# The order of expert dots, weights and sums at the start of a product-key expert stage, and the order of its row buffers

## The chip, the cores and the metric

The kernel is one program on one NeuronCore of a Trainium2 chip. The metric is the device time of one launch in microseconds (us). Three runs of the kernel before took 2640.28 us in the median (2638.99 to 2640.45). A core has five engines that matter here: TensorE (PE) for matrix products, VectorE (DVE), ScalarE (ACT), GpSimd (POOL) and SyncE (SP). Each runs its own list of instructions in order and waits for others at semaphores. Sixteen DMA engines move data between device memory and the on-chip memory.

## What is computed

Two blocks follow each other on 256 tokens of width 1024. The change touches only the end of the second one, a product-key expert layer:

```
q = (xc @ peer_wq).reshape(PEER_CHUNK, PEER_HEADS, 2, PEER_QDIM // 2)
s = jnp.einsum('chpd,hpkd->chpk', q, peer_keys)
sv, si = lax.top_k(s, PEER_TOPK)                       # 16 of 128 keys, twice per head
cand = sv[..., 0, :, None] + sv[..., 1, None, :]       # 256 pairs
top_s, pos = lax.top_k(cand, PEER_TOPK)                # 16 experts per head
gate = jax.nn.softmax(top_s, axis=-1)
act = jax.nn.gelu(jnp.einsum('chkd,cd->chk', peer_u[eidx], xc))
return jnp.einsum('chk,chkd->cd', (gate * act), peer_v[eidx])
```

There are 8 heads with 16 chosen experts each, so each token needs 128 rows of `peer_u` and 128 of `peer_v`, 1024 numbers in each. All is float32.

## The kernel before

The tokens are two tiles of 128 (t = 0 and 1). One "row" n, from 0 to 255, is one chosen expert of each of the 128 tokens of a tile: n = 128 t + 16 h + k for head h and choice k. A row is one indirect DMA (line 3484, issued by POOL) which gathers for each token 8 KB, its row of u and its row of v side by side, into one of 16 row buffers. Four rows are a group (`SLOT_GROUPS`, group b holds rows 4b to 4b+3), so there are 64 groups.

Each row goes through four engines:

- POOL issues the gather when its buffer is free, that is when the row that used it last has been summed (`rows_summed`).
- DVE multiplies the u half with the token (`slot_dots`, line 3324).
- ACT makes the gated activation and from it a diagonal matrix (`slot_weight`, lines 2713 to 2724, the diagonal is the last of them).
- PE multiplies the diagonal with the v half and adds to the output (`sums`, line 2379).

Ahead of the gathers stands the choice of the experts. PE computes queries (`tile_queries` for one tile, `query_chunk` for both tiles, line 1890) with four weight blocks of 2 MB, wq0 to wq3 (heads 0 and 1, 2 and 3, 4 and 5, 6 and 7), ACT copies them (lines 2683, 2689), PE computes the key scores, ACT copies these (line 2695), and DVE ranks (`rank`, from line 3236; `pair_up`, line 3253; `rank_pairs`, from line 3261; `choose`, from line 3292). `expert_gates` (ACT line 2708, DVE line 3312) is the softmax. The units of choice are: head 0 of tile 0, head 1 of tile 0, then two heads at a time. Unit 1 must be chosen before row 16 is gathered, unit 2 before row 32, unit 3 before row 64.

The four engines run lists written out by hand, and each list mixes the groups with the queries and scores of later heads. In the kernel before:

- DVE chooses unit 0 and unit 1, then takes group 0, group 1, `rank(2)`, group 2, the rest of unit 2 between groups 2, 3 and 4, and unit 3 between groups 8 to 12.
- ACT makes the weights of group 0 after the last query copy of wq1, groups 1 and 2 after the scores of wq1, then takes the copy of tile 1's wq0 queries, group 3, scores, groups 4 and 5, `query_pair(2, 0)`, groups 6 and 7, `query_pair(2, 1)`, group 8, `key_scores(2)`, group 9 and so on.
- PE sums groups 0 to 2 after the scores of wq1, then computes tile 1's wq0 queries, sums group 3, and then alternates one `query_chunk` of wq2 and wq3 with one group, 4+c and 8+c.

Buffers 0 to 4 are free at once, buffer 5 after tile 1's normalised input has been transposed, buffers 6 and 7 lie in the memory of wq1 and are free after its last query copy, buffers 8 and 9 lie in the memory of wq2 and are lent to rows 5 and 6 before wq2 is loaded, and come back after wq2's queries. Buffers 10 to 15 become free later. So after the first ten rows the gathers of rows 10 to 41 run with eight buffers. SP loads wq2 after row 6 is summed, and wq3 after tile 1's transposes (`h2_transposes(1)`).

Of the kernel before, what the change touches and what calls it, by code (L numbers as in the profile page):

```python
# [332 lines left out]
def build_program(nc, W1, V1, K1, W2_all, VV2, K2, R2, PU, PV, xin, cin, out):  # L333
# [1394 lines left out]
    behind_scores = [free2, free2 + 2 * D, free2 + 8 * D]  # L1728
    row_at = free_at_once + [behind_norm] + behind_query[1] + behind_query[2] + behind_query[3] + behind_scores
    NBUF = len(row_at)  # L1730
    first_bufs = [*range(5), 8, 9, 5, 6, 7] + [*range(8)] * 4 + [8, 9, *range(8)] * 2
    BEFORE_QUERY = [5, 6]
    cycle = [*range(8, 16), *range(8)]
    buf_of = (first_bufs + cycle * (TT * P // NBUF))[:TT * P]
    uses_before = [buf_of[:n].count(buf_of[n]) for n in range(TT * P)]
    user_before = [max((m for m in range(n) if buf_of[m] == buf_of[n]), default=None) for n in range(TT * P)]
# [140 lines left out]
    def _(pe):  # L1877
# [503 lines left out]
                        if half == 1 or n == TT * P - 1:  # L2381
                            last.then_inc(rows_summed.sem, 1)

        SCORED = {0: (0, 4), 1: (2, 3), 2: (5, 5), 3: (6, 6)}

        def score_products(g, t, chunks=range(4)):
            b = act_ring.open(pe, "sp")
# [36 lines left out]
        item_now["fresh"] = False  # L2424
        tile_queries(wq1, 0)
        tile_transposes(1)
        pe.wait_ge(*hT2_by_act.at(0, 3))
        tile_queries(wq1, 1)
        key_scores(1)
        sums([0, 1, 2])  # L2430
        tile_queries(wq0, 1)
        sums([3])
        key_scores(0, (1,))
        h2_transposes(1)
        pe.drain().then_inc(weights.used, 1)
        for c in range(4):
            query_chunk(2, c)
            sums([4 + c])
        key_scores(2)
        for c in range(4):  # L2440
            query_chunk(3, c)
            sums([8 + c])
        key_scores(3)
        sums(range(12, len(SLOT_GROUPS)))


    @block.scalar
    def _(act):
# [277 lines left out]
        def slot_weights(groups):  # L2726
            for b in groups:
                for n in range(*SLOT_GROUPS[b]):
                    slot_weight(n)
                if b % 8 == 3 and b // 8 + 2 < len(UNITS):  # L2730
                    expert_gates(b // 8 + 2)

        tile_root(0)
# [7 lines left out]
        expert_gates(0)  # L2741
        tile_queries(1, 0)
        tile_evac(1)
        expert_gates(1)
        tile_queries(1, 1)
        slot_weights([0])
        key_scores(1)
        slot_weights([1, 2])
        tile_queries(0, 1)
        slot_weights([3])  # L2750
        key_scores(0, (1,))
        h2_copies(1)
        slot_weights([4, 5])
        query_pair(2, 0)
        slot_weights([6, 7])
        query_pair(2, 1)
# [13 lines left out]
    def _(v):  # L2770
# [574 lines left out]
        choose_first(0)  # L3345
        add_out(1, 1)
        tile_norm(1)
        choose_first(1)
        expert_gates(0)
        expert_gates(1)  # L3350
        v.wait_ge(*h2_ready.at(0, 0))
        for b in range(len(SLOT_GROUPS)):
            if SLOT_GROUPS[b][0] == P:
                v.wait_ge(*h2_ready.at(0, 1))
            slot_dots(b)
            ahead = b // 8 + 2
            if ahead < len(UNITS):
                phase = b % 8 - (ahead == 2)
                if phase == 0:
                    rank(ahead)  # L3360
                elif phase == 1:
                    pair_up(ahead)
                    rank_pairs(ahead)
                elif phase == 2:
                    choose(ahead)
                elif b % 8 == 4:
                    expert_gates(ahead)
            if b == 36:
                add_experts(0)
# [4 lines left out]
    @block.gpsimd  # L3374
    def _(pool):
        layers_pool(pool)
        def ptt(o, a, b, op):
            return pool.tensor_tensor(o, a, b, op)  # L3378

        def unit_keys(h, d, dst, factor):  # L3380
            t = slice(starts(h)[d], starts(h)[d] + 64)
            if h:
                ptt(dst, kk[:, :, t], factor, ALU.mult)
            else:
                ptt(dst[:, 0:4, :], kk[:, 0:4, t], factor[:, 0:4, :], ALU.mult)
                ptt(dst[:, 4:8, :], kk_late[:, :, t], factor[:, 4:8, :], ALU.mult)

        def removal_raw(h):
            for d in range(2):
                unit_keys(h, d, ch2(Pm)[:, d, :, :], R1[h % 2][:, d, :, :])  # L3390
            pool.drain()

        def key_factors(h):
            for d in range(2):
                a = R1[h % 2][:, d, :, :]
                ptt(a, a, bc(V2["k_a"], 2, 64), ALU.mult)
            pool.drain()
            for d in range(2):
                a = R1[h % 2][:, d, :, :]
                ptt(a, a, bc(ka_rest, 2, 64), ALU.add)  # L3400
            pool.drain()

        def removal_keys(h):
            pool.wait_ge(*decays_ready.at(h))
            for head in range(2):
                rows_ = slice(64 * head, 64 * head + 64)
                ptt(QK[rows_, :, head, :], ch(Pm)[rows_, :, :], ch(r2)[rows_, :, :], ALU.mult)
            pool.drain()
            for d in range(2):
                unit_keys(h, d, ch2(Pm)[:, d, :, :], R0_before[h % 2][d])  # L3410
            pool.drain().then_inc(pq_ready.sem, 1)

        def keys_raw(h):
            for d in range(2):
                a = R1[h % 2][:, d, :, :]
                ptt(a, a, zk[:, :, starts(h)[d]:starts(h)[d] + 64], ALU.mult)
            pool.drain()

        def keys(h):
            raw = R1[h % 2].rearrange("p d c n -> p (d c) n")  # L3420
            for head in range(2):
                rows_ = slice(64 * head, 64 * head + 64)
                ptt(QK[rows_, :, 1 - head, :], raw[rows_, :, :], ch(r2)[rows_, :, :], ALU.mult)
            pool.drain().then_inc(k_ready.sem, 1)

        def begin_inverse(h):
            first = C2["level"].rearrange("p (m d t) -> p m d t", m=LEVELS + 1, d=2)[:, 0, :, :]
            for d in range(2):
                pool.wait_ge(*intra_ready.at(h, d))
                if h:  # L3430
                    pool.wait_ge(*u_ready.at(h - 1, d))
                for head in range(2):
                    rows_ = slice(64 * head, 64 * head + 64)
                    ptt(ch2(DTm)[rows_, d, :, :], ch2(LA[head])[rows_, d, :, :], bc(first[rows_, d, :], 1, 8), ALU.mult)
                pool.drain().then_inc(inverseT_ready[d].sem, 1)  # L3435

        for pair in range(8):
            d, c = divmod(2 * pair, 8)
            pool.wait_ge(*cumsum_ready.at(0, pair))
            for part in range(2):  # L3440
                pool.dma_start(rates_dram[d, :, :, part, c:c + 2, :].rearrange("b p c n -> p b (c n)"),  # L3441
                               staged[pair % 3][part].rearrange("p b c n -> p b (c n)")).then_inc(rates_stored[pair % 3], 16)
        pool.wait_ge(*kk_ready.at(0))
        pool.wait_ge(rates_landed[0], 64)
        pool.wait_ge(weights.used, used0 + SLOTS + LAST_BEFORE_SCAN + 1)
        removal_raw(0)
        key_factors(0)
        removal_keys(0)
        keys_raw(0)
        keys(0)  # L3450
        for h in STEPS:
            begin_inverse(h)
            if h == 0:
                pool.tensor_copy(kk[:, 4:8, :], kk_late)
                pool.drain()
            if h < 7:
                pool.wait_ge(rates_landed[(h + 1) % 2], 64 * ((h + 1) // 2 + 1))
                act_ring.peek(pool, "post", "U0", 2 * h + 1)
                if h in X_STEPS:
                    dve_ring.peek(pool, "post", "reads1", 2 * (h - 4) + 1)  # L3460
                removal_raw(h + 1)
                key_factors(h + 1)
                removal_keys(h + 1)
                keys_raw(h + 1)
                keys(h + 1)

        for n in range(TT * P):
            if n in UNIT_AT:
                pool.wait_ge(*experts_ready.at(0, UNIT_AT[n]))
            m, at = user_before[n], row_at[buf_of[n]]  # L3470
            if m is None and at == behind_norm:
                pool.wait_ge(*hT2_by_act.at(0, 3))
            for g, done in ((1, 3), (3, 6)):
                if m is None and at == behind_query[g][0]:
                    pool.wait_ge(*qTp_ready.at(0, done))
            if n == BEFORE_QUERY[0]:
                pool.wait_ge(weights.used, used0 + SLOTS + ITEM2["wq0"] + 1)
            elif m == BEFORE_QUERY[0]:
                pool.wait_ge(*qTp_ready.at(0, 5))
            if m is None and at == behind_scores[0]:  # L3480
                pool.wait_ge(*scores_ready.at(0, 8))
            if m is not None:
                pool.wait_ge(*rows_summed.at(0, m))
            pool.indirect_dma_start(out=rows_uv[buf_of[n]], out_offset=None, in_=UV,  # L3484
                                    in_offset=bass.IndirectOffsetOnAxis(ap=eidx_u[:, n:n + 1], axis=0)).then_inc(row_landed[buf_of[n]], 16)
# [32 lines left out]
```

## Time and profile before

| | |
|---|---|
| median of three runs | 2640.28 us |
| profiled execution, its own time | 2640.01 us |
| its span in the profile | 2638.1 us |
| PE busy | 2438.0 us (92%) |
| DVE busy | 1509.2 us (57%) |
| ACT busy | 899.9 us (34%) |
| POOL busy | 649.6 us (25%) |
| gathers of rows | 256, from 1960.0 to 2593.5 us |

The profile's page divides the span into 40 equal slices, 66 us each. The expert stage is the last ten of them. In the rows below a busy time has its own column, and the engine's idle time ahead of an instruction stands in brackets with what ended it: `[10.83 <-PE psum L2379]` says that the engine stood still for 10.83 us until an instruction of line 2379 on PE had finished. Line 2780 is a helper through which many DVE products and sums are issued.

### The profile page before, as it was taken

To read this page: it belongs to the slowest core of one execution; us is meant where nothing else is said; L and a number is where in the kernel's file an instruction comes from. 1 tells how busy PE (TensorE), PEld (TensorE's weight loads), DVE (VectorE), ACT (ScalarE), POOL (GpSimd) and SP (SyncE) were. 2 spreads that over 40 slices of the span, in tenths; PEclk is the share of its full clock that TensorE was granted. 3 is DMA by queue.
4 is the path that set the end of the run, shared out by engine and by line. 5 is a ranking of instruction groups with operands and counts; after the bars stand their busy time and mean duration, and the time that the engine had idled before them with its cause. 6 is when DMAs were issued, how large, how long until landed. Compare 5 with 4: busy or idle time off the path is not lost.

```text
span 2638.1 us, 48116 instructions
## 1 busy us (share of the span) xinstructions
PE 2438.0 (92%) x19036; PEld 1682.9 (64%) x19036; DVE 1509.2 (57%) x2848; ACT 899.9 (34%) x2505; POOL 649.6 (25%) x512
## 2 busy tenths in 40 slices
PE   8999999999999999999999888989999987877787
PEld 6588696476887954845677778888865532322232
DVE  1874376537734755576457445455056666677654
ACT  1252100013330000016332333221016676766676
POOL 0000014300000242000014657440013454444551
PEclk9999999999999999999999999999999999999999
DMA  4432444344234545215432111003449999999997
GB/s 186 156 128 97 160 160 160 147 175 150 106 124 180 224 160 206 114 64 224 158 130 64 34 23 30 19 34 137 159 181 393 414 421 421 421 422 421 421 421 301
DMA packets 91686, 523.98 MB, mean 199 GB/s; under 512 B 39776, under 2 KB 39776, under 8 KB 43488
## 3 DMA queue, kind: packets, MB, share of 16 engines
q0 software_dynamic: 39360, 277.51, 25.7%
q1 hardware_dynamic: 52128, 243.80, 24.8%
q8 instruction: 127, 2.08, 0.3%
q14 instruction: 71, 0.58, 0.1%
HBM read 511.85 MB, written 9.44 MB: 198 GB/s over the span
## 4 chain that ended last, share of the span: by engine, by line
PE 68%; DVE 11%; DMA 10%; issue 5%; ACT 3%; POOL 1%; POOLq 1%; DVEq 1%; ACTq 1%; PEldq 0%; SPq 0%
PE psum L571 34%; PE psum L1890 23%; DMA mem<-weights,mem 10%; PE psum L2379 5%; DVE mem L2780 4%; DVE mem L3324 3%; PE psum L813 2%; PE psum L587 1%; POOL mem L3378 1%; PE psum L2347 1%; DVE mem L3131 1%; PE psum L1900 1%; POOLq L3435 1%; ACT mem L2724 0%; ACT mem L2720 0%
## 5 line engine op out<-in xcount | busy, mean ns | idle before, releaser
L1890 PE MATMUL psum<-mem 64*64 64x64 f32 (+6 forms) x12356 | 874.4, 265 | 53.9 <-DVEq L3135 14.7
L571 PE MATMUL psum<-mem 128*128 128x128 f32 (+9 forms) x4856 | 910.4, 359 | 11.2 <-DVE mem L1198 3.5
L1890 PEld LDWEIGHTS psum<-mem 64*64 64x64 f32 (+4 forms) x12356 | 710.3, 151 | 208.1 <-issue 124.5
L571 PEld LDWEIGHTS psum<-mem 128*128 128x128 f32 (+4 forms) x4856 | 685.4, 183 | 230.5 <-issue 158.1
L2379 PE MATMUL psum<-mem 128*128 128x512 f32 x1024 | 505.3, 633 | 108.2 <-ACT mem L2724 108.0
L2379 PEld LDWEIGHTS psum<-mem 128*128 128x128 f32 x1024 | 187.5, 197 | 419.4 <-ACT mem L2724 259.2
L3324 DVE CUSTOM_DVE_ANT_0 mem<-mem 128x1024 f32<-128x1024 f32 x256 | 314.1, 1227 | 208.0 <-DMA mem<-weights,mem 191.3
L3484 POOL DMA_INDIRECT mem<-weights,mem x256 | 295.1, 1153 | 537.1 <-PE psum L2379 310.3
L2780 DVE TENSOR_TENSOR mem<-psum,mem 128x512 f32<-128x512 f32 (+2 forms) x180 | 111.5, 630 | 254.8 <-PE psum L1890 228.2
L3378 POOL TENSOR_TENSOR mem<-mem 128x512 f32<-128x512 f32 (+3 forms) x148 | 205.7, 1402 | 153.7 <-DVEq L3100 120.2
L2780 DVE TENSOR_TENSOR mem<-mem 128x512 f32<-128x512 f32 (+4 forms) x154 | 135.4, 893 | 11.8 <-ACTq L2540 2.2
L1552 POOL TENSOR_TENSOR mem<-mem 128x1024 f32<-128x1024 f32 x14 | 26.9, 1924 | 460.3 <-ACTq L1102 460.3
L1263 DVE SCALAR_TENSOR_TENSOR mem<-mem 128x256 f32<-128x256 f32 x240 | 105.6, 481 | 9.0 <-issue 0.4
L2724 ACT ACTIVATE mem<-mem 128x128 f32<-128x128 f32 x256 | 102.8, 402 | 18.5 <-issue 0.7
L2720 ACT ACTIVATE mem<-mem 128x1 f32<-128x1 f32 x256 | 99.1, 387 | 18.4 <-issue 0.3
L2715 ACT ACTIVATE mem<-mem 128x1 f32<-128x1 f32 x256 | 99.1, 387 | 18.1 <-issue 0.3
L3441 POOL DMA_DIRECT2D rates_dram<-mem x16 | 14.2, 891 | 366.8 <-DVEq L3018 366.8
L2642 ACT ACTIVATE mem<-psum 128x512 f32<-128x512 f32 x80 | 47.7, 597 | 130.6 <-PE psum L1890 130.6
L2713 ACT ACTIVATE mem<-mem 128x1 f32<-128x1 f32 x256 | 49.8, 195 | 119.8 <-DVEq L3325 118.8
L949 ACT ACTIVATE mem<-psum 128x512 f32<-128x512 f32 (+4 forms) x88 | 45.6, 569 | 104.4 <-PE psum L571 100.2
L1563 POOL MEMSET mem<- 128x256 f32 x1 | 0.3, 305 | 319.3 <-ACT mem L1097 319.3
L1101 ACT ACTIVATE mem<-mem 128x1024 f32<-128x1024 f32 x14 | 14.8, 1058 | 168.4 <-DVEq L1199 168.4
(284 smaller groups left out, 1791.9 us busy)
## 6 DMA issues: line engine op xcount, KB each, us to landing
mem<-weights SPq DMA_DIRECT2D x97, 2048.0 KB, 7.3
mem<-weights SPq DMA_DIRECT2D x13, 1024.0 KB, 9.9
rates_dram<-mem POOLq DMA_DIRECT2D x16, 512.0 KB, 5.0
mem<-rates_dram SPq DMA_DIRECT2D x32, 256.0 KB, 4.6
mem<-weights SPq DMA_DIRECT2D x2, 2176.0 KB, 7.9
mem<-weights,mem POOLq DMA_INDIRECT x256, 30.8
mem<-weights SPq DMA_DIRECT2D x2, 1536.0 KB, 8.1
mem<-weights SPq DMA_DIRECT2D x2, 1152.0 KB, 8.8
```

What stands on the lines that cost most here:

```text
L571: ins = pe.matmul(out, lhsT, rhs, start=start, stop=stop, skip_group_check=skip)
L813: ins = pe.matmul(b, mg[:, k, t * P:(t + 1) * P], w[half][:, k, :], start=k == 0, stop=k == 7)
L1263: v.scalar_tensor_tensor(cacc[:, c, :], src, w, cacc[:, c, :], ALU.mult, ALU.add)
L1890: ins = pe.matmul(out, lhsT, rhs, start=start, stop=stop, skip_group_check=skip)
L2379: last = pe.matmul(psum[:, 4 + 2 * t + half, :], diag[:, n % DIAGS, :], rows_uv[buf_of[n]][:, D + half * 512:D + (half + 1) * 512], start= ...
L2715: A(w, w, ACT.Identity, scale=dot, bias=dot)
L2720: A(w, w, ACT.Identity, scale=dot, bias=dot)
L2724: A(diag[:, n % DIAGS, :], ident, ACT.Copy, scale=w).then_inc(diag_ready.sem, 1)
L2780: return v.tensor_tensor(o, a, b, op)
L3324: v.tensor_tensor_reduce(u, u, h2[:, n // P, :], 1.0, 0.0, ALU.mult, ALU.add, actp[:, n:n + 1])
L3378: return pool.tensor_tensor(o, a, b, op)
L3484: pool.indirect_dma_start(out=rows_uv[buf_of[n]], out_offset=None, in_=UV, in_offset=bass.IndirectOffsetOnAxis(ap=eidx_u[:, n:n + 1], axis ...
```

## The change

PE, ACT and DVE get other lists for the first groups, and the row buffers are used in another order. No instruction's work is changed, except that one query product of 512 columns and its copy are cut into two halves.

- DVE takes group 0 after `rank(1)`, group 1 after `rank_pairs(1)`, and only then `choose(1)` and `expert_gates(1)`. Group 2 follows, then `rank(2)`; unit 2 lies one group later than before.
- ACT takes group 0 ahead of the copy of tile 1's wq1 queries, group 1 ahead of the scores of wq1, and group 2 behind `expert_gates(1)`. The copy of tile 1's wq0 queries is halved, with group 3 between the halves and group 4 behind. From `query_pair(2, 0)` on ACT's list is as before.
- PE sums group 0 ahead of tile 1's wq1 queries, group 1 ahead of the scores of wq1, group 2 behind them, group 3 between the halves of tile 1's wq0 queries and group 4 behind. From there on each `query_chunk` is followed by the group 5+c or 9+c, one later than before.
- Buffers 6 and 7 are used first by rows 11 and 12, not by rows 8 and 9. Rows 8, 9 and 10 take buffers 0, 1 and 2 again.

```diff
-    first_bufs = [*range(5), 8, 9, 5, 6, 7] + [*range(8)] * 4 + [8, 9, *range(8)] * 2
+    eight = [0, 1, 2, 6, 7, 3, 4, 5]
+    first_bufs = [*range(5), 8, 9, 5] + eight * 4 + [8, 9, *eight] * 2
-    cycle = [*range(8, 16), *range(8)]
+    cycle = [*range(8, 16), *eight]
...
         tile_queries(wq1, 0)
         tile_transposes(1)
+        sums([0])
         pe.wait_ge(*hT2_by_act.at(0, 3))
         tile_queries(wq1, 1)
+        sums([1])
         key_scores(1)
-        sums([0, 1, 2])
-        tile_queries(wq0, 1)
+        sums([2])
+        tile_queries(wq0, 1, (0, 1))
         sums([3])
+        tile_queries(wq0, 1, (2, 3))
+        sums([4])
         key_scores(0, (1,))
         h2_transposes(1)
         pe.drain().then_inc(weights.used, 1)
         for c in range(4):
             query_chunk(2, c)
-            sums([4 + c])
+            sums([5 + c])
         key_scores(2)
         for c in range(4):
             query_chunk(3, c)
-            sums([8 + c])
+            sums([9 + c])
         key_scores(3)
-        sums(range(12, len(SLOT_GROUPS)))
+        sums(range(13, len(SLOT_GROUPS)))
...
-                if b % 8 == 3 and b // 8 + 2 < len(UNITS):
+                if b % 8 == (3 if b >= 8 else 5) and b // 8 + 2 < len(UNITS):
                     expert_gates(b // 8 + 2)
...
         tile_evac(1)
+        slot_weights([0])
+        tile_queries(1, 1)
+        slot_weights([1])
+        key_scores(1)
         expert_gates(1)
-        tile_queries(1, 1)
-        slot_weights([0])
-        key_scores(1)
-        slot_weights([1, 2])
-        tile_queries(0, 1)
+        slot_weights([2])
+        tile_queries(0, 1, 0, 2)
         slot_weights([3])
+        tile_queries(0, 1, 2, 4)
+        slot_weights([4])
         key_scores(0, (1,))
         h2_copies(1)
-        slot_weights([4, 5])
+        slot_weights([5])
         query_pair(2, 0)
         slot_weights([6, 7])
         query_pair(2, 1)
...
-        choose_first(1)
+        rank(1)
         expert_gates(0)
+        v.wait_ge(*h2_ready.at(0, 0))
+        slot_dots(0)
+        pair_up(1)
+        rank_pairs(1)
+        slot_dots(1)
+        choose(1)
         expert_gates(1)
-        v.wait_ge(*h2_ready.at(0, 0))
-        for b in range(len(SLOT_GROUPS)):
+        for b in range(2, len(SLOT_GROUPS)):
...
-                phase = b % 8 - (ahead == 2)
+                phase = b % 8 - (2 if ahead == 2 else 0)
```

The remaining lines of the diff move the indices of `qTp_ready` by one, since the halved copy signals twice.

## Rows read from the trace of the kernel before

**Rows 1.** The page, 40 slices: busy tenths and GB/s of the DMA engines

```profile
DMA  4432444344234545215432111003449999999997
GB/s 186 156 128 97 160 160 160 147 175 150 106 124 180 224 160 206 114 64 224 158 130 64 34 23 30 19 34 137 159 181 393 414 421 421 421 422 421 421 421 301
```

**Rows 2.** Busy time by stretch: engines with instruction counts, PE's granted clock, DMA share, GB/s

```profile
1972.00:1974.00 2.00, 2.00 (x11) 2.00 (x11) 1.65 (x5) 0.00 (x0) 0.00 (x0) 0.50 1.01 426
...
2018.00:2020.00 2.00, 2.00 (x5) 0.68 (x4) 1.74 (x3) 1.73 (x7) 1.31 (x1) 1.00 0.06 25
2020.00:2022.00 2.00, 2.00 (x5) 0.68 (x4) 1.84 (x3) 1.72 (x7) 1.09 (x2) 1.00 0.65 143
...
2020.00:2060.00 40.00, 39.74 (x133) 23.80 (x133) 16.56 (x30) 29.35 (x102) 15.66 (x16) 1.00 0.99 399
...
2100.00:2200.00 100.00, 86.81 (x199) 35.46 (x197) 70.04 (x159) 72.22 (x257) 51.23 (x48) 0.95 1.01 421
```

**Rows 3.** DVE in order of time, the dot of the last row

```profile
2628.23 1.23 DVE L3324 CUSTOM_DVE_ANT_0 mem<-mem 128x1024 f32<-128x1024 f32 x1 [1.22 <-DMA mem<-weights,mem]
```

**Rows 4.** POOL in order of time: start, duration; issues of rows 0, 8 and 20

```profile
1960.03 1.07 POOL L3484 DMA_INDIRECT mem<-weights,mem  x1 [197.34 <-DVE mem L3303]
...
1979.87 0.95 POOL L3484 DMA_INDIRECT mem<-weights,mem  x1 [8.82 <-ACTq L2685]
...
2018.69 1.45 POOL L3484 DMA_INDIRECT mem<-weights,mem  x1 [10.83 <-PE psum L2379]
```

**Rows 5.** DVE in order of time, 1963 to 2025 us

```profile
1963.98 0.49 DVE L3236 MAX8 mem<-mem 128x8 f32<-128x128 f32 x2
...
1967.01 0.18 DVE L3253 CAST mem<-mem 128x32 f32<-128x32 uint32 x1
...
1970.12 0.20 DVE L3292 TENSOR_SCALAR mem<-mem 128x16 uint32<-128x16 uint32 x1
...
1974.40 0.17 DVE L3312 TENSOR_REDUCE mem<-mem 128x1 f32<-128x16 f32 x1
...
1975.97 1.22 DVE L3324 CUSTOM_DVE_ANT_0 mem<-mem 128x1024 f32<-128x1024 f32 x1 [0.18 <-issue]
1977.36 1.23 DVE L3324 CUSTOM_DVE_ANT_0 mem<-mem 128x1024 f32<-128x1024 f32 x1 [0.16 <-issue]
...
1988.08 0.87 DVE L3236 MAX8 mem<-mem 128x8 f32<-128x128 f32 x4 [1.13 <-ACTq L2697]
...
1993.62 1.23 DVE L3324 CUSTOM_DVE_ANT_0 mem<-mem 128x1024 f32<-128x1024 f32 x1
...
2024.76 1.23 DVE L3324 CUSTOM_DVE_ANT_0 mem<-mem 128x1024 f32<-128x1024 f32 x1 [1.72 <-DMA mem<-weights,mem]
```

**Rows 6.** ACT in order of time: query copies and the first weights

```profile
1978.97 0.60 ACT L2683 ACTIVATE mem<-psum 128x512 f32<-128x512 f32 x1 [4.41 <-PE psum L1890]
1979.68 0.20 ACT L2713 ACTIVATE mem<-mem 128x1 f32<-128x1 f32 x1
...
1981.33 0.40 ACT L2724 ACTIVATE mem<-mem 128x128 f32<-128x128 f32 x1
...
1983.26 0.40 ACT L2724 ACTIVATE mem<-mem 128x128 f32<-128x128 f32 x1
...
2013.63 0.60 ACT L2683 ACTIVATE mem<-psum 128x512 f32<-128x512 f32 x1 [9.22 <-PE psum L1890]
```

**Rows 7.** PE in order of time: queries and scores L1890, sums L2379

```profile
1969.89 10.92 PE L1890 MATMUL psum<-mem 128*128 128x128 f32 x80 [2.86 <-ACTq L2680]
...
2006.29 7.31 PE L1890 MATMUL psum<-mem 128*128 128x128 f32 x64
...
2067.74 5.40 PE L1890 MATMUL psum<-mem 128*128 128x128 f32 x32
2072.98 7.03 PE L2379 MATMUL psum<-mem 128*128 128x512 f32 x16
2079.84 3.62 PE L1890 MATMUL psum<-mem 128*128 128x256 f32 x16
```

More of the change, by code:

```diff
@@ L2382, in sums @@
                             last.then_inc(rows_summed.sem, 1)
-        SCORED = {0: (0, 4), 1: (2, 3), 2: (5, 5), 3: (6, 6)}
+        SCORED = {0: (0, 5), 1: (2, 3), 2: (6, 6), 3: (7, 7)}
         def score_products(g, t, chunks=range(4)):
@@ L3365, in _ @@
                     choose(ahead)
-                elif b % 8 == 4:
+                elif phase == 4:
                     expert_gates(ahead)
@@ L3472, in _ @@
                 pool.wait_ge(*hT2_by_act.at(0, 3))
-            for g, done in ((1, 3), (3, 6)):
+            for g, done in ((1, 3), (3, 7)):
                 if m is None and at == behind_query[g][0]:
@@ L3478, in _ @@
             elif m == BEFORE_QUERY[0]:
-                pool.wait_ge(*qTp_ready.at(0, 5))
+                pool.wait_ge(*qTp_ready.at(0, 6))
             if m is None and at == behind_scores[0]:
```

## The prediction, made before the changed kernel was run

> **What bounds the kernel now.** I read the page's slices first [rows 1]. From the 31st slice on, 1979 us, the DMA engines are full at 414 to 422 GB/s to the end. The stretches say the same more sharply: share 1.01 and 421 GB/s in 2100 to 2200 us [rows 2]. A row is 128 x 8 KB = 1.049 MB, so it costs 1.049 MB / 421 GB/s = 2.49 us, and 256 rows are 637 us of the 678 us that lie between the first gather [rows 4] and the end. The last dot waits for a gather too [rows 3]. So the expert stage is bound by DMA from its first gather to its last, and only two things can move the time: when the first gather starts, and how long the DMA engines stand empty in between.
>
> The first gather starts at 1960.03, released by `choose(0)` [rows 4]. The change puts nothing ahead of that. Inside the stage I looked for stretches under full share. There is one: 0.06 and 0.65 in 2018 to 2022 [rows 2], that is 1.9 + 0.7 = 2.6 us of standstill. It is the wait of row 20 for its buffer: POOL idle for 10.83 us until a sum on PE had ended, issue at 2018.69 [rows 4]. Behind it stand ACT, idle 9.22 us until the copy at 2013.63 [rows 6], and PE, which had to finish 7.31 us of queries from 2006.29 first [rows 7]. After the hole the gathers depend on PE: it is busy 39.74 of 40 us in 2020 to 2060 [rows 2], with sums of 7.03 us and query pieces of 3.62 us end to end [rows 7].
>
> **What the change can gain.** The hole and no more: 2.6 us, with its edges about 3. That would give 2640.0 - 3 = 2637. What the trace doesn't show is the changed order itself, so I lay the four lists out by hand with durations of this profile.
>
> **Unit costs.** A dot 1.39 us, from start to start [rows 5]. The first diagonal is ready 1981.33 + 0.40 - 1979.68 = 2.05 us after ACT begins, each further one 1.93 us later [rows 6]. A group of sums takes 7.03 us with ready diagonals, 4 x 1.93 = 7.7 at ACT's pace. `rank(1)` 3.0, `rank_pairs(1)` 3.1, `choose(1)` with its gate shift 4.3, `rank(2)` 5.5 us, by the differences of starts [rows 5]. A query product of 512 columns 7.31 us, a chunk of both tiles 3.6, two score products 5.40 - 3.6 = 1.8, so 0.9 each [rows 7]; a copy 0.6 [rows 6]. From issue to the dot of a row on an empty queue 2024.76 - 2018.69 = 6.1 us [rows 4, 5], so row n lands at about 1966 + 2.5 n at first. Two further numbers concern the queue. A weight block is 2.1 MB, two rows. And the pace at which rows come to the dots is a little slower than 2.49: from row 20 to row 255 with wq3 between, (2628.23 - 2024.76) / 237 = 2.55 us [rows 3, 5]. I use 2.55.
>
> **The first three groups.** DVE: dots of group 0 from 1967.8, paced by the landings until 1975, then 3.1 us of pairs, group 1 until row 7 has landed, 1985, `choose(1)` until 1989. ACT has finished tile 1's transposed copies at 1969.9 (where PE's wait of 2.86 us ended, [rows 7]); weights of group 0 from 1970 to 1978. PE sums them 1972 to 1979.7. Only then come tile 1's wq1 queries, 7.3 us, before at 1969.89 [rows 7], now until 1987; copy until 1987.6. Row 11, the first in the wq1 buffers, is issued then. The rows ahead of it, 0 to 10, keep the queue full until about 1962 + 11 x 2.5 = 1989.5, so this is just in time: cost 0 to 1 us. Weights of group 1, ready since 1979, now stand behind that copy: 1987.6 to 1995.4, sums until 1997, two scores until 1998.8, copies until 1999.3. ACT's `expert_gates(1)` is behind them and DVE waits for it before group 2: dots from 2000.3, where they were at 1993.62 [rows 5]. `rank(2)` no longer stands ahead of them, which gives 5.5 us of DVE back, but DVE has idled 11 us. Sums of group 2 run from 2003.7 to 2011.2, half a query until 2014.8, copy and first weight, sums of group 3 from 2017.3. Row 20 waits for row 12 as before, so the hole stays: issue at 2019.5 instead of 2018.69, 3 us empty.
>
> **The loop behind.** Here is the dearest part. From `query_pair(2, 0)` on ACT's list is unchanged, while PE has moved one group forward. Before, group 5 is weighted ahead of the copy of the first wq2 pair and summed behind it, so PE finds its diagonals ready and never stops. After, the sums of group 6 come directly behind chunk 1, whose copy stands ahead of ACT's group 6: PE waits 0.6 + 2.05 = 2.65 us, and again at groups 8, 10 and 12; the halved query costs 0.4 + 2.05 at groups 3 and 4 in the same way. The scores of wq2 stand behind the sums of group 8 and not of 7, and `rank(3)`, which waits for them, stands ahead of the dots of group 9: scores copied at 2090, rank until 2095.7, dots, weights, sums from 2099. Written out, the sums of groups 3 to 12 begin at 2017.3, 2030.8, 2043.9, 2057.3, 2068.2, 2081.3, 2099.0, 2112.7, 2123.7, 2136.7. In the trace group 8 begins at 2072.98 [rows 7].
>
> **The sum.** With eight buffers, four rows are issued as four are summed. From group 3 to group 12 that is 119.4 us for 36 rows. The queue needs 36 x 2.55 = 91.8 for them, 5.1 for wq3, and 5.1 for the two rows that come on top when buffers 8 and 9 return. It stands empty for 119.4 - 102.0 = 17.4 us, plus the first hole of 3.1, together 20.5; laid out row by row, since a hole can't be saved up, 19.9. The same reckoning for the kernel before, whose groups 3 to 12 take 98 us, gives no hole but the first, 2.1 us at this pace (2.6 to 3 by the stretches). Difference +17.8. After row 64 all 16 buffers are in use and the full queue hides everything in both. The end behind the last row (10 us) is the same. The profiled execution took 2640.0 (span 2638.1 and 1.9 around it, 0.3 under the median): 2640.0 + 18 = 2658.
>
> **The clock.** After PE's wait of 2.86 us the first 64 instructions took 9.1 us (1969.89 to the copy at 1978.97 [rows 6, 7]) where 2006.29 has 7.31, and the granted clock was 0.50, the 1.2 GHz level, in 1972 to 1974 [rows 2]: 1.8 us for one drop. After the change PE idles 4.9 us ahead of the first diagonal and about 5 ahead of group 9. The first drop is partly hidden, since ACT paces that group; another would lie on the path. Taken as two drops that is up to +3.6. The Trainium skill, "TensorE: Matmul & The Clock Gate", Part 1, states that an idle TensorE falls to its lower clock and that activity releases it. The trace agrees (0.50); by it the shorter gaps could cost as well, which the row at 2006 to 2016 doesn't show.
>
> **The rivals.** (A) The hole is filled: halved queries and early dots bring row 20's buffer back in time and PE finds its diagonals. Then the time is 2637. For it speaks that the hole is made by one 7.31 us product in one piece; against it that group 3 can't be summed before 2017 with DVE held by `expert_gates(1)`. It holds if row 12 is summed before 2015. (B) A part only: the start costs 1 to 3 us, and backlog in the queue swallows the PE waits of 2.65 us, as PE's busy share of 87% after 2100 shows some slack [rows 2]. Then about 2640 + 1 + 5 = 2646, for the rank of unit 3 alone. Against it: eight buffers are 20 us, one group's round trip with dots, weights and sums. (C) My layout plus both clock drops and a later group 9: 2640 + 18 + 6 = 2664. (D) The end on the other side through buffers alone: if the buffer order lets gathers start earlier, the gain still can't pass A's bound.
>
> **How the numbers follow.** Forecast (2651 to 2661) 0.60, C 0.15, B 0.12, A and D 0.13. Likeliest 2658. The range 2645 to 2667 leaves out A and the far ends. A measurement of this kernel can tell about 0.2%, 5.3 us. Faster than 2634.7 lies beyond A's bound and needs something I haven't seen: 0.03. Within 0.2% are A and the weak end of B: 0.11. Slower 0.86.
>
> **What would show it.** Right: DVE idle for about 11 us ahead of the ninth dot, released by ACT's gates; PE idle some 2.6 us ahead of groups 6, 8, 10 and 12; the MAX8 of `rank(3)` released by a score copy near 2090; DMA share under 1 around 2018, 2031, 2097 and 2113; row 64 issued some 18 us later. Wrong: DMA share full after 2022 although PE idles, which would mean that the backlog is deeper than eight rows.

## The result and the profile after

The changed kernel takes 2662.88 us in the median of six runs (2659.57 to 2670.09), the kernel before 2640.36 (2636.09 to 2641.76). The ratio is 1.0091, 95% interval 1.0075 to 1.0106: slower by 22.5 us. I had forecast 2658, slower, with a range of 2645 to 2667.

The page's slices, DMA share and GB/s:

```profile
DMA  5332344443234545215532110013468899999997
GB/s 189 151 127 103 152 159 159 165 160 153 96 127 178 221 176 201 95 68 220 188 108 53 33 35 19 18 52 153 171 251 351 330 392 421 421 422 421 421 421 307
```

Before, the 31st and 32nd slices moved 393 and 414 GB/s and the queue was full from the 33rd on [rows 1]; the prediction put the full rate one slice too early, for the 31st has 393. Now the 31st to 33rd slices move 351, 330 and 392 GB/s, and it is full only from the 34th, 2193 us.

POOL in order of time: the first gather, row 11, row 20, row 24, row 46 and row 64 of the changed kernel:

```profile
1954.44 1.07 POOL L3497 DMA_INDIRECT mem<-weights,mem  x1 [196.59 <-DVE mem L3311]
...
1983.16 0.94 POOL L3497 DMA_INDIRECT mem<-weights,mem  x1 [7.99 <-ACTq L2690]
...
2017.30 0.95 POOL L3497 DMA_INDIRECT mem<-weights,mem  x1 [6.43 <-PE psum L2380]
...
2031.28 0.95 POOL L3497 DMA_INDIRECT mem<-weights,mem  x1 [6.82 <-PE psum L2380]
...
2102.46 0.95 POOL L3497 DMA_INDIRECT mem<-weights,mem  x1 [13.23 <-PE psum L2380]
...
2150.18 0.95 POOL L3497 DMA_INDIRECT mem<-weights,mem  x1 [0.30 <-issue]
```

The first gather starts 5.6 us earlier than in the profile before [rows 4]. That is not the change: over the kernels measured below it lies anywhere between 1952.7 and 1963.9, without order. So I compare by **stage**, the time from the start of the first gather to the end of the span in the profiled execution: 2638.1 - 1960.0 = 678.1 before, 2657.8 - 1954.4 = 703.4 after, +25.3. Times after the first gather are written "at +n". Row 20 is issued at +62.9, before at +58.7, and row 64 at +195.7, before at 2127.63 - 1960.03 = +167.6.

One stage is one profiled execution, and its scatter was not measured. Two versions below give an idea of it. They have the same lists behind group 3 and issue row 64 at the same +173.7, and their stages still differ by 1.4 us. And the difference of a version's stage from the stage before lies up to 4 us from the difference of the medians. Differences of 1 or 2 us between two stages are therefore not told apart from scatter here.

PE in order of time, sums of groups 0, 2, 3, 6, 8, 9 and 10:

```profile
1966.44 8.63 PE L2380 MATMUL psum<-mem 128*128 128x512 f32 x16 [5.00 <-ACT mem L2729]
...
1999.85 8.99 PE L2380 MATMUL psum<-mem 128*128 128x512 f32 x16 [5.16 <-ACT mem L2729]
2008.68 3.73 PE L1891 MATMUL psum<-mem 128*128 128x128 f32 x32
2015.04 7.79 PE L2380 MATMUL psum<-mem 128*128 128x512 f32 x16 [2.63 <-ACT mem L2729]
...
2055.82 7.78 PE L2380 MATMUL psum<-mem 128*128 128x512 f32 x16 [2.62 <-ACT mem L2729]
...
2080.22 7.78 PE L2380 MATMUL psum<-mem 128*128 128x512 f32 x16 [2.84 <-ACT mem L2729]
2087.85 5.40 PE L1891 MATMUL psum<-mem 128*128 128x128 f32 x32
2098.41 9.21 PE L2380 MATMUL psum<-mem 128*128 128x512 f32 x16 [5.16 <-ACT mem L2729]
...
2113.69 1.98 PE L2380 MATMUL psum<-mem 128*128 128x512 f32 x4 [2.62 <-ACT mem L2729]
```

Line 2380 is the sums, 1891 queries and scores. Where the kernel before went from sums to queries to sums without a bracket [rows 7], groups 3, 4, 6, 8, 9, 10 and 12 now have one that names ACT's diagonal.

DVE in order of time, the gates of unit 1 and the first instruction of `rank(3)`:

```profile
1995.68 0.17 DVE L3320 TENSOR_REDUCE mem<-mem 128x1 f32<-128x16 f32 x1 [11.58 <-ACT mem L2713]
...
2089.60 0.87 DVE L3244 MAX8 mem<-mem 128x8 f32<-128x128 f32 x4 [15.37 <-ACTq L2702]
```

And the largest hole by stretches (engines, granted clock, DMA share, GB/s):

```profile
2096.00:2098.00 2.00, 0.00 (x0) 0.00 (x0) 1.68 (x5) 1.41 (x6) 0.00 (x0) 0.50 0.83 344
2098.00:2100.00 2.00, 1.59 (x2) 0.83 (x3) 1.84 (x3) 1.73 (x7) 0.00 (x0) 0.50 0.09 37
2100.00:2102.00 2.00, 2.00 (x4) 0.69 (x3) 1.80 (x6) 1.73 (x7) 0.00 (x0) 0.50 0.00 0
2102.00:2104.00 2.00, 2.00 (x5) 0.89 (x4) 1.85 (x10) 1.73 (x7) 0.95 (x1) 0.84 0.00 0
```

`rank(3)` waits 15.37 us for the scores of wq2, the dots of group 9 stand behind it, PE waits 5.16 us for their diagonals, and the queue is all but empty from 2098 to 2104; row 46 is issued at 2102.46. That is the dearest single place.

### The profile page after: what moved, and what is told of

Same layout as the page of the kernel before. It is cut to its first block, busy times and chain, and to the rows that moved or that the text cites. A ratio compares the mean times of both kernels' runs of the same rounds, so it can differ in the third digit from the quotient of the medians.

```text
span 2657.8 us, 48117 instructions
## 1 busy us (share of the span) xinstructions
PE 2438.7 (92%) x19036; PEld 1679.2 (63%) x19036; DVE 1508.7 (57%) x2848; ACT 899.6 (34%) x2506; POOL 657.0 (25%) x512
## 4 chain that ended last, share of the span: by engine, by line
PE 70%; DVE 11%; DMA 8%; issue 4%; ACT 2%; POOL 1%; DVEq 1%; POOLq 1%; ACTq 0%; PEldq 0%; SPq 0%
PE psum L571 34%; PE psum L1891 24%; DMA mem<-weights,mem 8%; PE psum L2380 7%; DVE mem L2788 4%; DVE mem L3332 3%; PE psum L813 2%; PE psum L587 1%; PE psum L2348 1%; POOL mem L3391 1%; DVE mem L3139 1%; PE psum L1901 1%; POOLq L3448 1%; ACT mem L2729 0%; POOL mem L3497 0%
## 5 line engine op out<-in xcount | busy, mean ns | idle before, releaser
L3497 POOL DMA_INDIRECT mem<-weights,mem x256 | 302.4, 1181 | 554.4 <-PE psum L2380 317.7
L2729 ACT ACTIVATE mem<-mem 128x128 f32<-128x128 f32 x256 | 102.8, 402 | 18.2 <-issue 0.3
```

Of the source, the lines that this page charges most:

```text
L2729: A(diag[:, n % DIAGS, :], ident, ACT.Copy, scale=w).then_inc(diag_ready.sem, 1)
```

## The experiments

All versions were timed beside the kernel before. The ratios carry the scatter of the first gather's start, so I read the size of an effect from the stage in the profile, and its sign from both.

**The parts of the change.** First the changed front with the loop as it was:

```diff
# against the changed kernel
-        sums([4])
...
-            sums([5 + c])
+            sums([4 + c])
...
-            sums([9 + c])
+            sums([8 + c])
...
-        slot_weights([4])
         key_scores(0, (1,))
         h2_copies(1)
-        slot_weights([5])
+        slot_weights([4, 5])
```

> The changed kernel, but with the loop as before: on PE each query chunk of wq2 and wq3 is followed by group 4+c and 8+c again, and ACT weights group 4 behind the copies of tile 1's transposes. The front (groups 0 to 3, the halved query, the buffers) stays changed. Theory A (the loop's order costs most: PE has moved one group forward and ACT has not): my layout gives a time 3.6 us over the kernel before, 2644 us; holes of DMA remain near 2018 and 2031 on the clock of the kernel before, and PE finds diagonals ready from group 5 on. Theory B (the late front is the cause, DVE's wait of some 11 us ahead of the ninth dot, and the loop only hands it on): the time stays near the changed kernel, 2655 to 2663.

Measured: ratio 1.0041 (1.0027 to 1.0055), 2646.6 us against 2636.1 beside it. Stage 685.5 us, +7.4. "Front" here includes the halved query and the buffer order. Its size is twice my 3.6, but 18 of the 25 us are gone, and from group 5 on PE runs without a bracket, as theory A says:

```profile
2041.81 7.03 PE L2380 MATMUL psum<-mem 128*128 128x512 f32 x16
...
2052.13 7.03 PE L2380 MATMUL psum<-mem 128*128 128x512 f32 x16
```

Then the loop moved alone, front and buffers as before:

```diff
# against the kernel before
-        sums([3])
+        sums([3, 4])
...
-            sums([4 + c])
+            sums([5 + c])
...
-            sums([8 + c])
+            sums([9 + c])
...
-        slot_weights([3])
+        slot_weights([3, 4])
...
-        slot_weights([4, 5])
+        slot_weights([5])
```

> The kernel before with only the loop moved: PE sums group 4 right behind group 3 and then group 5+c and 9+c behind each chunk, ACT weights group 4 behind group 3. Front and buffers as before. Theory A: 12.7 us over the kernel before by the layout, 2653 us, and up to 2 more if TensorE's clock falls ahead of group 9; the waits of 2.6 us ahead of groups 6, 8, 10 and 12 and the late rank(3) are there. Theory B: within 3 us of the kernel before.

Measured: ratio 1.0080 (1.0063 to 1.0097), stage 699.2 us, +21.1. Theory B is out: with an untouched front the loop alone brings five sixths of the loss. The size was 12.7 in the layout, too small. PE, groups 8, 9 and 10:

```profile
2068.00 8.83 PE L2379 MATMUL psum<-mem 128*128 128x512 f32 x16 [2.84 <-ACT mem L2724]
2076.67 5.40 PE L1890 MATMUL psum<-mem 128*128 128x128 f32 x32
2087.24 10.06 PE L2379 MATMUL psum<-mem 128*128 128x512 f32 x16 [5.17 <-ACT mem L2724]
...
2103.38 8.83 PE L2379 MATMUL psum<-mem 128*128 128x512 f32 x16 [2.62 <-ACT mem L2724]
```

The two parts add to 28.5, the whole is 25.3. That they share waits would explain it, but I have not taken it apart.

**The buffers alone.**

```diff
# against the kernel before
-    first_bufs = [*range(5), 8, 9, 5, 6, 7] + [*range(8)] * 4 + [8, 9, *range(8)] * 2
+    eight = [0, 1, 2, 6, 7, 3, 4, 5]
+    first_bufs = [*range(5), 8, 9, 5] + eight * 4 + [8, 9, *eight] * 2
...
-    cycle = [*range(8, 16), *range(8)]
+    cycle = [*range(8, 16), *eight]
```

> The kernel before with only the new order of the row buffers. Row 8 then waits for the sum of row 0 (about 1983.9 in the trace) where it waited for a copy (1979.87). Layout: the queue has rows 0 to 7 until about 1982, so a new hole of 3.3 us opens near 1983, and the hole near 2018 closes since everything behind is later by as much: 1.3 us over the kernel before, 2641.6 us. Rival (the buffer order is what costs, since it takes two rows of lead away for good): 5 us or more over the kernel before.

Measured: ratio 1.0002 (0.9992 to 1.0011), stage 676.9 us, -1.2. By stretches:

```profile
1982.00:1984.00 2.00, 2.00 (x6) 0.74 (x5) 1.68 (x5) 1.73 (x7) 0.82 (x1) 1.00 0.65 270
1984.00:1986.00 2.00, 2.00 (x5) 0.68 (x5) 1.84 (x3) 1.72 (x7) 1.23 (x2) 1.00 0.54 107
2016.00:2018.00 2.00, 2.00 (x5) 0.68 (x4) 1.78 (x4) 1.73 (x7) 0.17 (x1) 1.00 0.99 414
2018.00:2020.00 2.00, 2.00 (x6) 0.70 (x5) 1.85 (x3) 1.66 (x7) 1.01 (x2) 1.00 1.02 426
```

As laid out, the hole moves from 2018 [rows 2] to 1983 and does not double. The new hole is 1.6 us by share (2.2 us by rate) and not 3.3. On the kernel before, the buffer order costs nothing that the ratio can tell, about 0.1% at most; on the changed front it was not measured by itself.

**DVE's long wait.** The front has one wait that looks like the culprit, 11.58 us. This version takes it away from the dots:

```diff
# against the changed kernel
         choose(1)
-        expert_gates(1)
...
             slot_dots(b)
+            if b == 2:
+                expert_gates(1)
```

> The changed kernel, but DVE takes expert_gates(1) behind the dots of group 2 and not ahead of them, so that the dots of group 2 do not wait for ACT's exponential. Theory A: DVE's wait of 11.6 us is mostly hidden behind ACT and PE, which are not ready either; 2 us less than the changed kernel, about 2660. Theory B: the wait is the cause, and 8 us or more come back, 2654 or less.

Measured: ratio 1.0100 (1.0083 to 1.0117), 2663.2 us, stage 704.0 us, nothing gained; both forecasts, 2660 and 2654, were too low. The sums of group 2 begin at +43.2 and not +45.4, the 2 us of the layout, but they then take 10.11 us:

```profile
2003.94 10.11 PE L2380 MATMUL psum<-mem 128*128 128x512 f32 x16 [2.96 <-ACT mem L2729]
```

The mean granted clock over these sums was 0.70, against 0.79 in the changed kernel. Group 3 takes 8.79, and row 20 is issued at +63.5 against +62.9. So slower sums at the lower clock took back the 2 us. The wait for the gates is 5.49 us here and stands behind the dots of group 2. The 11.58 us, long as they are, are not what the loss hangs on: with the dots freed of them, the sums of group 2 start only 2 us earlier.

**Where the layout was too short.** My first thought was TensorE's clock after the new waits. I filled the waits with products whose results nobody reads (fillers):

```diff
# against the changed kernel
+        def keep_busy(count):
+            for i in range(count):
+                pe.matmul(psum[:, 7, 0:P], ident, ident, start=True, stop=True)
...
+        keep_busy(36)
         sums([0])
...
+        keep_busy(36)
         sums([2])
...
             query_chunk(3, c)
+            if c == 0:
+                keep_busy(36)
```

> The changed kernel with 36 additional products of 128 columns on PE, whose results nobody reads, in each of the three places where PE idled about 5 us: ahead of the sums of groups 0, 2 and 9. They take some 4 us each and end before the diagonals are ready. In the changed kernel these three groups took 8.63, 8.99 and 9.21 us where ACT's pace gives 7.7, and the granted clock was at 0.50 there. Theory C (the part of the loss that my layout missed, some 7 us, is in good part TensorE's lower clock after the new waits): the three groups go back to 7.8 us and the stage from first gather to end takes 699 to 701 us and not 703.4. Rival (the missed part has nothing to do with the clock): 703 to 704 us.

Measured: ratio 1.0129 (1.0113 to 1.0144), stage 709.0 us. This one shows nothing about the clock: a float32 product is two instructions in the profile, the 36 took 8.2 us and not 4, and held up each of the three groups by 3 us. The same mistake is in the next, which fills the waits of the loop moved alone:

```diff
# against the loop moved alone
             query_chunk(2, c)
+            if c in (1, 3):
+                keep_busy(18)
...
             query_chunk(3, c)
+            if c != 2:
+                keep_busy(40 if c == 0 else 18)
```

> The loop moved alone, as measured before (stage 699.2 us, 21.1 over the kernel before where the layout gave 12.7), with additional products of 128 columns on PE whose results nobody reads: 18 behind chunks 1 and 3 of wq2 and chunks 1 and 3 of wq3, 40 behind chunk 0 of wq3. They fill the new waits of 2.6 and 5.2 us. Theory C: the granted clock stays at 1.00 there, groups 8, 9 and 10 take 7.8 us and not 8.83, 10.06 and 8.83, and the stage shortens to 691 to 694 us, near the layout's 678.1 + 12.7 = 690.8. Rival: 698 to 700 us, the layout was too short for another reason.

Measured: ratio 1.0079 (1.0063 to 1.0094), stage 699.1 us. Inconclusive, since the fillers again ran over the waits. Repeated with counts that fit, 20 for each 36:

> As the first kept-busy version of the changed kernel, but with 20 additional products in each of the three places and not 36. The 36 took 8.2 us, 0.114 us for each of their 72 instructions, and so held up the sums by 3 us in each place; 20 take 4.6 us and end before the 5.0 to 5.2 us of the waits. Theory C: the three groups take 7.8 us, and the stage is 699 to 701 us (changed kernel 703.4). Rival: 703 to 704.

Measured: ratio 1.0091 (1.0057 to 1.0124), stage 702.5 us, 0.9 less than without fillers. PE, filler and group 2, then groups 1 and 10:

```profile
2001.11 4.63 PE L2411 MATMUL psum<-mem 128*128 128x128 f32 x40
2006.44 7.78 PE L2380 MATMUL psum<-mem 128*128 128x512 f32 x16 [0.70 <-ACT mem L2737]
...
1990.66 8.83 PE L2380 MATMUL psum<-mem 128*128 128x512 f32 x16 [2.84 <-ACT mem L2737]
...
2117.65 8.83 PE L2380 MATMUL psum<-mem 128*128 128x512 f32 x16 [2.62 <-ACT mem L2737]
```

Filled groups 2 and 9 take 7.8 us as expected (group 0 8.3, with a short wait inside), but now groups 1 and 10, behind unfilled waits of 2.6 to 2.8 us, take 8.83. The ratio is that of the changed kernel, 1.0091. And the loop alone, with 11 and 21 fillers:

> As the first kept-busy version of the loop moved alone, with 11 additional products (2.5 us) in the waits of 2.6 to 2.8 us and 21 (4.8 us) in that of 5.2 us ahead of group 9; before, they took 4.2 and 9.1 us and held up the sums. Theory C: granted clock 1.00 around groups 8 to 10, stage 691 to 694 us (loop alone 699.2, layout 690.8). Rival: 698 to 700 us.

Measured: ratio 1.0059 (1.0032 to 1.0085), stage 697.4 us, 1.8 less than without fillers. Groups 8 and 9 are back at 7.8 and group 10 at 8.1, and groups 3 and 4 together take 17.00 us where they took 15.70. But groups 3 and 4 lie ahead of the first filler, so the fillers did not slow them. PE ahead of the first filler, first the loop alone, then the version with fillers, in the same order:

```profile
1962.57 10.92 PE L1890 MATMUL psum<-mem 128*128 128x128 f32 x80 [2.87 <-ACTq L2680]
...
2009.11 15.70 PE L2379 MATMUL psum<-mem 128*128 128x512 f32 x32 [2.84 <-ACT mem L2724]
```

```profile
1970.60 12.17 PE L1890 MATMUL psum<-mem 128*128 128x128 f32 x80 [2.87 <-ACTq L2688]
...
2018.40 17.00 PE L2379 MATMUL psum<-mem 128*128 128x512 f32 x32 [2.84 <-ACT mem L2732]
```

The same products behind the same waits are 1.3 us longer in one execution than in the other, twice, and group 5 begins at +80.2 and not +77.7. From group 5 to group 12 the version with fillers needs 94.4 us where the loop alone needs 98.4: there 4.0 us came back, where the slow sums of groups 8 to 10 had cost 8.83 + 10.06 + 8.83 - 3 x 7.8 = 4.3, but this execution had lost 2.5 before the first filler. Last, the changed front with the loop as before:

```diff
# against the changed front with the loop as before
+        keep_busy(20)
         sums([0])
...
+        keep_busy(20)
         sums([2])
```

> The changed front with the loop as before (stage 685.5 us, 7.4 over the kernel before where the layout gave 3.6), with 20 additional products ahead of the sums of groups 0 and 2. Theory C: groups 0 and 2 take 7.8 us and not 8.65 and 9.00, and 2 to 3 us of the 7.4 come back: stage 682.5 to 683.5. Rival: 685 to 686.

Measured: ratio 1.0024 (1.0009 to 1.0039), stage 684.1 us, 1.4 less. Group 3 takes 8.83 instead, and row 64 is issued at +173.7 as without fillers. In all three pairs the stage is shorter, by 0.9, 1.8 and 1.4 us where I expected 2 to 8, but none of this stands clear of scatter: the ratios are 1.0091 and 1.0091, 1.0080 and 1.0059, 1.0041 and 1.0024, and in each pair the intervals overlap. What fillers bring to the whole stage is not shown. What the traces do show is that the place of a fall is not fixed by the list. The two versions with 20 fillers have the same list up to group 3; in one group 1 takes 8.83 and group 3 7.79 us, in the other group 1 takes 7.84 and group 3 8.83.

**Is it the lead, or the groups' new place?** In this version the groups stay forward, and PE takes each chunk one group earlier, so chunks lead groups as in the kernel before:

```diff
# against the changed kernel
-        for c in range(4):
-            query_chunk(2, c)
-            sums([5 + c])
+        query_chunk(2, 0)
+        for c in range(1, 4):
+            query_chunk(2, c)
+            sums([4 + c])
         key_scores(2)
         for c in range(4):
             query_chunk(3, c)
-            sums([9 + c])
+            sums([8 + c])
         key_scores(3)
-        sums(range(13, len(SLOT_GROUPS)))
+        sums(range(12, len(SLOT_GROUPS)))
```

> The changed kernel, but PE computes each query chunk of wq2 and wq3 one group earlier (chunk 0 and chunk 1 of wq2 ahead of group 5, then one chunk ahead of each group, the scores of wq2 behind group 7). The groups keep their new place ahead of tile 1's last scores, only the lead of chunks over groups is that of the kernel before. Theory A (the loss is the lost lead and nothing else in the loop): the waits ahead of groups 6, 8, 9, 10 and 12 are gone; layout 5.9 us over the kernel before, and with what the layout missed in the front up to 10; stage 684 to 688 us. Rival (moving the groups forward is itself dear, since group 4 holds up the load of wq3): 695 us or more.

Measured: ratio 1.0052 (1.0036 to 1.0067), stage 687.8 us, +9.7 and not +25.3. A change on PE's list alone gives back 15.6 us of stage. By the ratios it is 1.0091 against 1.0052, about 10 us, and the intervals (1.0075 to 1.0106, 1.0036 to 1.0067) are apart. The groups' new place is kept, only the lead is restored, so most of the loss in the loop is the lost lead. The second and third stretch of 60 us behind the first gather show where it comes back:

```profile
2021.31:2081.31 60.00, 56.94 (x217) 35.55 (x216) 30.39 (x56) 39.46 (x134) 24.07 (x21) 1.00 0.94 354
2081.31:2141.31 60.00, 58.71 (x169) 29.57 (x168) 46.13 (x115) 41.06 (x144) 30.55 (x28) 1.00 1.01 422
```

The changed kernel has 353 and 332 GB/s there (shown below). The second stretch, with the waits ahead of groups 6 and 8, is no better. One chunk more stands ahead of group 5, which begins at +91.6 and not +88.1, and at group 8 this version is only 1.4 us ahead, +124.4 against +125.8. From group 8 to group 12 it is 40.9 us, as in the kernel before, against 58.1. The largest piece of that is the step from group 8 to group 9, 10.3 against 18.2 us, where the late `rank(3)` stood.

**A version meant to beat both.** The gap of the kernel before is PE's one piece of 7.31 us ahead of group 3 [rows 7]. Cut it and put the halves into waits that are there anyway:

```diff
# against the kernel before
-        sums([0, 1, 2])
-        tile_queries(wq0, 1)
+        sums([0])
+        tile_queries(wq0, 1, (0, 1))
+        sums([1, 2])
+        tile_queries(wq0, 1, (2, 3))
         sums([3])
...
         slot_weights([1, 2])
-        tile_queries(0, 1)
+        tile_queries(0, 1, 0, 2)
         slot_weights([3])
+        tile_queries(0, 1, 2, 4)
```

(with the indices of `qTp_ready` moved by one as in the change)

> A version meant to beat both: the kernel before, with tile 1's wq0 queries computed in two halves, the first behind the sums of group 0, the second behind those of group 2, and copied by ACT behind group 2 and group 3. Nothing else moves. Layout: PE fills waits it has anyway, ACT no longer idles 9.2 us ahead of group 3, row 20 gets its buffer some 3 us earlier, the hole near 2018 closes, nothing opens: 2 us under the kernel before, 3 at most, so 2638; the stage takes 675 to 676.5 us. If the hole only moves to another group, the stage stays at 678.

Measured: 2634.67 us against 2637.19 beside it (twelve and seventeen runs), ratio 0.9992, interval 0.9983 to 1.0000. That can't be told from no change, so it isn't shown that this version beats the kernel before. Stage 673.7 us, -4.4, more than the 2 of the layout; by the medians it is 2.5 us. The first 60 us, from 4 us behind the first gather, in the kernel before, this version and the changed one:

```profile
1964.03:2024.03 60.00, 51.96 (x236) 31.83 (x235) 50.24 (x151) 33.26 (x113) 21.23 (x20) 0.97 0.96 392
```

```profile
1960.58:2020.58 60.00, 54.66 (x268) 37.06 (x267) 50.37 (x151) 37.10 (x125) 22.07 (x21) 0.97 1.01 416
```

```profile
1958.44:2018.44 60.00, 44.36 (x196) 27.09 (x194) 39.87 (x128) 31.10 (x105) 19.58 (x18) 0.91 0.93 375
2018.44:2078.44 60.00, 53.27 (x186) 30.44 (x184) 30.32 (x56) 32.52 (x112) 21.49 (x20) 1.00 0.91 353
2078.44:2138.44 60.00, 47.37 (x145) 26.23 (x145) 40.28 (x106) 30.85 (x107) 20.71 (x18) 0.94 0.85 332
2138.44:2198.44 60.00, 55.09 (x127) 21.82 (x128) 38.75 (x100) 46.06 (x163) 36.47 (x33) 0.97 0.98 402
```

The version meant to beat both has a full queue from the start: 416, 420, 421 and 421 GB/s over its four stretches.

## Why the prediction was right, and where its sizes were off

**The bound.** Right. A lower mean rate than 421 GB/s is time lost by the queue: over four stretches of 60 us behind the first gather, 60 x (421 - GB/s) / 421 adds to 31.6 us after (375, 353, 332, 402) and 5.7 before (392, 409, 422, 421). The difference is 25.9, the stage grew by 25.3. The same sum fits these versions within 1.5 us, and the other six too:

| version | stage less that of before | loss of the queue less that of before |
|---|---|---|
| changed kernel | +25.3 | +25.9 |
| loop moved alone | +21.1 | +22.2 |
| chunks ahead | +9.7 | +10.3 |
| changed front, loop as before | +7.4 | +7.7 |
| buffers alone | -1.2 | -2.7 |
| halves in gaps | -4.4 | -4.8 |

This is an account of where time went, not a cause: every version moves the same rows, so a longer stage must show as a lower rate. The cause is that gathers are issued late. After row 64 both kernels have a full queue, as the prediction has it.

**The first three groups.** Right in order and nearly in time. Sums of group 0 at +12.0 (layout +12.0), group 1 at +30.6 (+29.4), group 2 at +45.4 (+43.7). The wait for the gates is 11.58 us, where I had 11; row 20 is issued at +62.9 where I had +59.5, and the hole stays, as forecast. That DVE's wait has next to no share in the loss was not in the prediction; the version with the gates later shows it.

**The loop behind.** Right: PE's waits ahead of groups 3, 4, 6, 8, 10 and 12 are 2.62 to 2.84 us where I had 2.65 (2.45 at groups 3 and 4), ahead of group 9 5.16 where I had 5. `rank(3)` waits for the score copy, at +135.2 where I had +130. The four holes forecast are there, near +64, +78, +147 and +162 where I had +58, +71, +137 and +153, and there are two more, near +106 (the wait ahead of group 6) and +187 (group 12). The version with chunks ahead shows that most of this is the lead and not the groups' new place, and rivals A and B are out: PE's waits are not swallowed. The share of the parts is as I put it, the loop first; but "the dearest part" is even dearer, 21.1 alone against 7.4 for the front alone.

**The sum, too small by 7 us.** I had +17.8, the stage shows +25.3. Two terms of the layout were too short. The way from group 3 to group 12 was 119.4 us and is 2138.37 - 2015.04 = 123.3, 3.9 more. And group 3 was to begin at +57.3 and begins at +60.6, 3.3 more. So group 12 begins at +183.9 where the layout had +176.7. Two things are in these 7.2 us. The groups at the lower clock (0, 2 and 9) took 8.63, 8.99 and 9.21 us and not 7.8, which makes 3.4 us; I had priced that beside the forecast and not in it. The rest, 3.8 us, is spread in pieces of up to 0.5 us over most steps of the layout: from the start of group 3 to that of group 4 it says 13.5, the trace 14.0. That these are handovers between engines which my unit costs leave out is my guess; no version isolates them. Row 64, which I had some 18 us later, is 28 us later. Here too my holes were too small in both kernels: 19.9 and 2.1 us, where the sum above gives 31.6 and 5.7.

**Where the number was lucky.** The profiled execution took 2659.6 us, next to my 2658, though its stage was 7.5 us longer than forecast. Its first gather started 5.6 us earlier than in the profile before, and that hid most of the miss. The median of six, 2662.9, lies 4.9 us over the forecast.

**The clock.** I allowed up to 3.6 us for two drops, beside the forecast. There were three, and their 3.4 us of longer sums are in the measured time. Whether they can be had back is open: with the long waits filled, only 0.9 us of stage came back, which is within scatter, and groups 1 and 10 ran at a mean granted clock of 0.81 behind two shorter waits instead. That gaps of 2.6 to 2.8 us can cost too is what the prediction weighed with "TensorE: Matmul & The Clock Gate", Part 1, of the Trainium skill, by which an idle TensorE falls to its lower clock, and said the row at 2006 to 2016 doesn't show. The loop moved alone shows it without any filler, 8.83 us behind a wait of 2.84, while the changed kernel has 7.78 behind a wait just as long at group 8. So a gap of that length sometimes costs 1 us and sometimes nothing. Rival C, 2664, is nearer to the median than my 2658; its mechanism, clock drops beside the layout, covers 3.4 of the missing 7 us at most.

**The buffers and what can be gained.** The bound of 3 us for the hole was too low by the stage: the version with halves in gaps has 4.4 us less, though the medians differ by 2.5 and the ratio can't be told from 1. Before, the stretch of 2020 to 2022 had share 0.65 but 143 GB/s, a third of full rate [rows 2]. I counted by share, 2.6 us; by rate, 2018 to 2022 loses 2 x (396 + 278) / 421 = 3.2 us, and all four stretches behind the first gather lose 5.7.

**What stays open.** How much of the 22.5 us between the medians is noise of the earlier stages: the first gather's start scatters by some 11 us over the profiles, and the stage says 25.3. I have not taken apart the 3.8 us that are not the clock, nor, inside the lost lead, the late `rank(3)` from PE's waits at groups 10 and 12. And 9.7 us remain with the lead restored; the changed front has 7.4 of them by the version with the loop as before, and its group 3 begins at +60.6 where it began at +56.4. Which of the moved items in the front makes this is not shown: putting the gates later brought nothing, and neither the buffer order nor the halved query cost anything on the kernel before.

## What to carry to other kernels

Where several engines run hand-written lists in step, moving one item forward on one list shifts its lead against all the others. Check the whole loop behind it, not the place that was edited: a product, its copy and the next group's weights must not come to stand in a row. In a stage bound by a queue, ask what the next eight buffers wait for. Of the versions that move work on PE's list, only the one that moves it into waits that are already there (halves of the 7.31 us piece) didn't cost anything. And a long wait need not be a dear one: moving the 11.58 us on DVE brought nothing, while restoring the lead, which removes PE's repeated waits of 2.6 us and the late rank, brought 15.6 us of stage, about 10 by the ratios.

## What the runs showed of the hardware

- A queue that restarts after a hole counts as busy before it moves data at full rate. In the changed kernel:

```profile
2030.00:2032.00 2.00, 1.83 (x5) 0.67 (x4) 1.84 (x3) 1.72 (x7) 0.72 (x1) 1.00 0.26 107
2032.00:2034.00 2.00, 2.00 (x5) 0.68 (x4) 1.78 (x4) 1.72 (x7) 0.80 (x2) 1.00 0.55 106
2034.00:2036.00 2.00, 2.00 (x5) 0.68 (x4) 1.23 (x2) 0.85 (x3) 1.39 (x2) 1.00 0.97 410
```

  Share 0.55 went with 106 GB/s, a quarter of the full rate. Holes should be sized by GB/s.
- Whether TensorE's clock is low behind a short wait differs between executions of the same list. Behind a wait of 2.86 or 2.87 us the same 80 instructions took 9.29 us (buffers alone), 10.66 (halves in gaps), 10.92 (kernel before and loop alone) and 12.17 (loop alone with 11 and 21 fillers), though PE's list is the same up to there in all five; the granted clock stood at 0.50 in 1972 to 1974 of the kernel before [rows 2]. Of the two versions with 20 fillers, one has 8.83 us for group 1 behind a wait of 2.84, at a mean granted clock of 0.81, the other 7.84 at 1.00.
- A product of two float32 matrices counts as two instructions on PE in the profile: 36 products of 128 columns are 72 instructions and took 8.2 us.
